# Rows of 1/rms through DRAM in place of TensorE's transposes, in a two-layer encoder

## The reference, cut to what matters

```
def rms_norm(x, g):
    y = x * rsqrt(mean(x * x, axis=-1) + EPS)
    return y * g
for l in range(2):
    x = x + hybrid_mixer(rms_norm(x, norm_mix_g[l]), ...)         # conv, attention, gMLP branches
    x = x + mem_cross_attention(rms_norm(x, norm_xattn_g[l]), mem, norm_mem_g[l], ...)
    x = x + conv_ffn(rms_norm(x, norm_ffn_g[l]), ...)             # up, depthwise conv, gate, down
return rms_norm(x, norm_final_g)
```

## Time and profile before

| | |
|---|---|
| median of 3 runs | 1756.15 us (1756.13 to 1756.55) |
| span of the profiled execution, first to last instruction | 1754.5 us |
| PE matmul busy | 1746.8 us, 8231 instructions |
| DVE busy | 1269.8 us |
| ACT busy | 744.8 us |
| POOL busy | 487.5 us |

### The profile page before, as it was taken

How to read it: one execution, slowest core, us unless ns; L and a number is a source line. 1 busy time by engine, 2 the same in 40 slices (tenths; PEclk the granted TensorE clock), 3 DMA queues, 4 the chain that set the end, 5 groups by cost and what they waited for, 6 DMA issues and landing times.

```text
span 1754.5 us, 21902 instructions
## 1 busy us (share of the span) xinstructions
PE 1746.8 (100%) x8231; PEld 1454.1 (83%) x8231; DVE 1269.8 (72%) x1688; ACT 744.8 (42%) x967; POOL 487.5 (28%) x204
## 2 busy tenths in 40 slices
PE   9999999999999999999999999999999999999998
PEld 7888888888888888888888888888888888888888
DVE  7998767573678777577779787665746797585585
ACT  4234654343564443343432345543445544343343
POOL 4453000103034244444133620010030333444440
PEclk9999999999999999999999999999999999999999
DMA  6532222322322332232231312223222223322321
GB/s 216 192 120 73 103 103 96 127 90 97 119 82 87 122 116 79 98 115 85 107 144 72 145 69 106 103 97 120 97 97 96 97 99 118 121 72 97 120 75 70
DMA packets 30698, 185.97 MB, mean 106 GB/s; under 512 B 3709, under 2 KB 6013, under 8 KB 10241
## 3 DMA queue, kind: packets, MB, share of 16 engines
q1 hardware_dynamic: 28380, 172.71, 27.4%
q0 software_dynamic: 1648, 11.54, 1.7%
q10 hardware_dynamic: 564, 0.33, 0.1%
HBM read 179.25 MB, written 7.68 MB: 107 GB/s over the span
## 4 chain that ended last, share of the span: by engine, by line
PE 96%; DVE 2%; issue 1%; ACT 1%; POOL 0%; DVEq 0%; POOLq 0%; ACTq 0%
PE ps L1640 28%; PE ps L1656 28%; PE ps L1641 28%; PE ps L1582 2%; PE ps L1576 2%; PE ps L1575 2%; PE ps L1739 1%; PE ps L1759 1%; DVE merged L1202 1%; DVE x_tl L985 1%; PE ps L1751 0%; PE ps L1670 0%; PE ps L1891 0%; PE ps L1884 0%; PE ps L1885 0%
## 5 line engine op out<-in xcount | busy, mean ns | idle before, releaser
L1640 PE MATMUL ps<-x_hd,w_hd 128*128 128x512 f32 x1568 | 612.8, 391 | 0.2
L1641 PE MATMUL ps<-x_tl,w_hd 128*128 128x512 f32 x1568 | 610.4, 389 | 0.0
L566 POOL TENSOR_TENSOR w_tl<-raw,w_hd 128x2048 fp32r<-128x2048 f32 x79 | 366.1, 4634 | 534.4 <-ACT w_hd L684 400.7
L684 ACT ACTIVATE w_hd<-raw 128x2048 fp32r<-128x2048 f32 (+2 forms) x159 | 298.2, 1876 | 324.8 <-PE ps L1641 240.3
L1656 PE MATMUL ps<-x_hd,w_tl 128*128 128x512 f32 x1568 | 373.4, 389 | 0.0
L1640 PEld LDWEIGHTS ps<-x_hd,w_hd 128*128 128x128 f32 x1568 | 294.4, 188 | 62.5 <-issue 0.8
L1656 PEld LDWEIGHTS ps<-x_hd,w_tl 128*128 128x128 f32 x1568 | 294.1, 188 | 61.0
L1641 PEld LDWEIGHTS ps<-x_tl,w_hd 128*128 128x128 f32 x1568 | 294.4, 188 | 60.3
L1640 PE MATMUL ps<-ring_hd,w_hd 128*128 128x512 f32 (+1 forms) x640 | 241.1, 381 | 0.0
L1641 PE MATMUL ps<-ring_tl,w_hd 128*128 128x512 f32 (+1 forms) x640 | 239.8, 379 | 0.0
L1347 DVE SCALAR_TENSOR_TENSOR merged<-merged 128x512 f32<-128x512 f32 x44 | 183.3, 4166 | 20.7 <-ACT merged L684 20.3
(11 more groups left out here) (227 smaller groups left out, 1646.1 us busy)
## 6 DMA issues: line engine op xcount, KB each, us to landing
raw<-units SPq DMA_DIRECT2D x154, 1024.0 KB, 4.8
bias_t<-bias_tiles POOLq DMA_DIRECT2D x8, 256.0 KB, 5.5
cg<-mem_t POOLq DMA_DIRECT2D x2, 1024.0 KB, 6.8
resid<-x_t POOLq DMA_DIRECT2D x1, 2048.0 KB, 8.2
resid_dram<-resid POOLq DMA_DIRECT2D x1, 2048.0 KB, 9.1
resid<-resid_dram POOLq DMA_DIRECT2D x1, 2048.0 KB, 8.8
out<-resid SPq DMA_DIRECT2D x7, 256.0 KB, 2.7
resid<-x_t SPq DMA_DIRECT2D x3, 512.0 KB, 9.0
```

What stands on the lines that cost most here:

```text
L566: line.done(pool.tensor_tensor(w_tl[:, k % 2, :], raw[:, k % 2, :], w_hd[:, k % 2, :].bitcast(F32), ALU.subtract), of_unit("tail", g))
L684: line.done(act.activation(out, in_, func, **kw), *labels)
L1640: pe.matmul(dst, w_hd[:, slot, w], hd[:, src, :], start=kc == 0, stop=False)
L1641: i = pe.matmul(dst, w_hd[:, slot, w], tl[:, src, :], start=False, stop=False)
```

## The change

For seven of the eight such places (`n0` of layer 1, and `c`, `mem` and `r2` of both layers) PE's `spread` is left out. In its place SP writes the columns element by element to a row in DRAM (`row_dram`), waits until the write has landed, and reads the row back broadcast to all 128 partitions. DVE waits for the read's semaphore `row_in`. DVE's copies of `misc` at `n0` of layer 1 and at `r2` go, and `c_norm` and the memory's scaling read the row in SBUF (`tmp[:, 3, :]`). `ROW_AT` says ahead of which unit's load SP does it. Layer 0's `n0` and the final norm keep the transposes.

```
+ROW_AT = {(0, 19): "c", (0, 31): "mem", (0, 48): "r2", (1, 4): "n0", (1, 19): "c", (1, 31): "mem", (1, 48): "r2"}
+ROW_NUMBER = {(_l, _tag): _n + 1 for _n, ((_l, _), _tag) in enumerate(ROW_AT.items())}
...
+        row = tmp[:, 3, :]
+        ROW_TO = {"n0": (rs0, r0[:], TB), "c": (rs, row, TB), "mem": (rs, row, MB), "r2": (rs, r_all, TB)}
+        row_dram = nc.dram_tensor("row_dram", (2, S), F32).ap()
...
+            def spread_row(tag):
+                src, dst, n = ROW_TO[tag]
+                number = ROW_NUMBER[line.part, tag]
+                sp.wait_ge(gpsimd_done, line.at(f"{tag}_rs"))
+                sp.dma_start(row_dram[number % 2, 0:P * n].rearrange("(t p) -> p t", p=P), src[:, 0:n],
+                             allow_slow_non_contiguous=True).then_inc(row_out, 16)
+                sp.wait_ge(row_out, 16 * number)
+                sp.dma_start(dst[:, 0:P * n], row_dram[number % 2, 0:P * n].rearrange("(o s) -> o s", o=1)
+                             .to_broadcast([P, P * n])).then_inc(row_in, 16)
+
             for g in range(2, TOTAL):
+                line.begin(g // NU)
+                if divmod(g, NU) in ROW_AT:
+                    spread_row(ROW_AT[divmod(g, NU)])
                 sp.wait_ge(gpsimd_done if tail_by_pool(g - 2) else vector_done, line.at(of_unit("tail", g - 2)))
                 sp.dma_start(raw[:, g % 2, :], units[g]).then_inc(weights_in[g % 2], 16)
...
-                op(lambda: dve.tensor_copy(r0[:], misc), "n0_r", needs=("n0b",))
+                if l:
+                    dve.wait_ge(row_in, 16 * ROW_NUMBER[l, "n0"])
+                else:
+                    op(lambda: dve.tensor_copy(r0[:], misc), "n0_r", needs=("n0b",))
...
-                                op(lambda: dve.tensor_copy(r_all, misc), "n2_r", needs=("r2b",))
+                                dve.wait_ge(row_in, 16 * ROW_NUMBER[l, "r2"])
...
+                        dve.wait_ge(row_in, 16 * ROW_NUMBER[l, "c"])
...
-                            op(lambda: dve.tensor_tensor(view, view, misc, ALU.mult), f"c_norm{t}", needs=("cb",))
+                            op(lambda: dve.tensor_tensor(view, view, row, ALU.mult), f"c_norm{t}")
...
-                    if k == CLN + 2:
-                        spread("c", 4)
...
-                        spread("mem", MB)
...
-                    if k == 44:
-                        spread("r2", 4)
```

More of the change, by code:

```diff
@@ L170 @@
 SUMS_IN = (2, 0)
-SPREAD_AT = (None, 1)
 IN_UNIT_2 = (5, 7)
@@ L451, in build @@
         out_sent = sem("out_sent")
+        row_out, row_in = sem("row_out"), sem("row_in")
         vector_waited, gpsimd_waited = sem("vector_waited"), sem("gpsimd_waited")
@@ L1401, in _ @@
                            "mem_ms", needs=("mems",))
+                    if k in MEM_SPLIT:
+                        dve.wait_ge(row_in, 16 * ROW_NUMBER[l, "mem"])
                     for t0 in MEM_SPLIT.get(k, ()):
@@ L1404, in _ @@
                             op(lambda: dve.scalar_tensor_tensor(sq[:, t % 2, 0:MEM], memf[:, t, :], col(l, "g_mem", t),
-                                                                misc[:, 0:MEM], ALU.mult, ALU.mult), f"mem_src{t}",
-                               needs=("memb",))
+                                                                row[:, 0:MEM], ALU.mult, ALU.mult), f"mem_src{t}")
                         for t in (t0, t0 + 1):
@@ L1843, in _ @@
                                 conv_sums if k == CLN + 2 and e == FIRST_OF[k] else
-                                first_spread if k == SPREAD_AT[l] else None)
-                        sums_at = KD // 2 if k == 39 else 2 if sums is first_spread or g == 2 else None
+                                None)
+                        sums_at = KD // 2 if k == 39 else 2 if g == 2 else None
                         if (kind, arg) == ("sv", 0):
@@ L1860, in _ @@
                         column_sums("mem", (), mem_sums, MB)
-                    if k == 27:
-                        pe.wait_ge(vector_done, line.at("ot3"))
-                        spread("mem", MB)
                     if k == 36:
```

## The result

The changed kernel takes 1783.76 us (median of 4 runs, 1782.52 to 1785.12) against 1756.14 for the kernel before on the same chip: 1.0157 times as long, 95% interval 1.0144 to 1.0169. The forecast was 1755.9, with a range up to 1759.4. It is slower, in the direction of the rival "a slow scatter" and beyond that rival's own upper bound of 1768.

A forecast was written before the change was run, and what follows sets the result against it. PE, busy 96% of the span, was taken to bound the kernel. Removed transposes (−2.64 us) plus late rows at `r2` (+2.4) gave −0.2, a median of 1755.9 us, with a range of 1753.4 to 1759.4.

The forecast's parts named there:

- a slow scatter: Rival: 512 writes of 4 bytes cost more than the load in front hides; slower, 1759.7 to 1768 us; chance 0.13.
- landing of the element write: At `r2`, SP's write to DRAM lands at 529.2, 0.7 us behind the load; bounds 528.46 and 532.1.
- The queue in front: At `r2`, the write stands behind a load with 2.6 us still to run, so it lands no earlier than 528.46.
- The read: The 256 KB broadcast read of the row takes 2.9 us; bounds 2.7 and 3.7.
- R: Time from the end of POOL's power until DVE may use the row; 6.4 us at `r2`, bounds 5.4 and 10.1.
- the prediction's formula: Time is 1753.5 + 2 × (R − 5.2) + 1 to 2 × (R − 7.6), brackets below zero counted as zero.
- 5.2 at `r2`: R beyond which each us delays PE by one us per layer, at unit (0, 52); 2.4 us in all at R = 6.4.
- 7.6 at `c`: R beyond which PE stalls for the evacuation ahead of unit (0, 17), one us per us; cost 0 at R = 6.4.
- DVE's fixed cycle: Behind `r2`, DVE and ACT run 10.58 us a unit against PE's 10.9, so DVE regains only 0.3 us a unit.
- a stall in units 45 to 47: Sign of being wrong: PE already stalls there, behind `r2`, rather than near the start of unit 52.
- Off PE: Removed transposes take 2.64 us off PE: 0.44 at each `r2`, `c` and `n0`, 0.22 at each `mem`.
- the fourth rival: The 24 transposes cost PE their duration of 0.27 us each, 6.5 us off PE; 1752 us; chance 0.05.

The follow-up runs named there:

- early, read alone: Against early: SP also waits for the row's read to land before issuing the next load; 1754.83 us (ratio 0.999).
- after: The changed kernel itself, with seven rows written to DRAM element by element; 1783.76 us (ratio 1.0157).
- pieces of 16 bytes, other order: Against the changed kernel: each partition writes its four numbers as one 16-byte piece, so tokens stand in another order; 1757.75 us (ratio 1.0008).
- 512 apart: Against the changed kernel: the 4-byte writes go 512 bytes apart in DRAM, and the read takes a row of weights; 1756.64 us.
- 64 apart: As 512 apart, but the 4-byte writes go 64 bytes apart in DRAM; 1756.59 us.
- 16 apart: As 512 apart, but the 4-byte writes go 16 bytes apart in DRAM; 1758.87 us.
- all in pieces: Against the changed kernel: all seven rows written in 16-byte pieces (8 at `mem`) in right order, PE turning every fourth (second) token's sums; 1757.53 us (1.0007).
- early: Against all in pieces: SP makes each row one unit earlier in its order, with no load in front in the queue; 1757.92 us (ratio 1.0009).
- PE kept busy: Against the changed kernel: useless matmuls added where PE waits, 16 at `c` and 22 at `r2`; 1789.3 us (ratio 1.0195).
- nothing in front: Against the changed kernel: SP makes each row one unit earlier, so no load runs in the queue when the write is issued; 1793.54 us.
- row in SBUF: Against the changed kernel: columns go element by element to one SBUF partition, then a second DMA copies them to the other 127; 1802.85 us (1.0265).
- kernels that turn every fourth token: Against the changed kernel: PE turns every fourth token's sums (second at `mem`), so each partition writes neighbours as one piece; four kernels, 1757.53, 1755.13, 1757.92, 1754.83 us.

## Why the prediction was wrong, step by step

**The step that failed** is the landing of the element write: taken at 529.2, 3.4 us after its issue, with 532.1 as the upper bound from the load of 128 elements at 3.66 us. It is 8.6 (7.98 to 9.9), outside both bounds. That row was no neighbour in the sense that matters: it reads single elements from DRAM and writes to SBUF, while this one writes 16 numbers into each 64 bytes of DRAM, and there the runs with distances put 5.5 us. The queue in front, from which I drew the lower bound, is worth 1.4 us (2.8 against 1.4 with pieces). The read was mis-sized too: 4.2 to 6.1 at `r2` and `c` against 2.9, its bounds 2.7 and 3.7.

**The rest of the sum held.** With each execution's R (end of the power to DVE's first use, from the rows of POOL and DVE) the prediction's formula, one us per us beyond 5.2 at `r2` and beyond 7.6 at `c` in each layer, gives the column "sum", where its 1753.5 is replaced by 1754.5. That constant is fitted to the fastest kernel, so the first row below is no test of it; where the 1.0 lies is in the next paragraph.

| kernel | R at `c`, layers 0 and 1 | R at `r2` | sum | measured |
|---|---|---|---|---|
| early, read alone | 5.4, 6.8 | 5.3, 5.3 | 1754.7 | 1754.83 (profiled: 1755.68) |
| after | 14.7, 14.6 | 12.8, 12.4 | 1783.4 | 1783.76 |
| pieces of 16 bytes, other order | 6.4, 6.7 | 6.8, 7.0 | 1757.9 | 1757.75 |
| 512 apart | 6.5, 6.3 | 6.1, 6.3 | 1756.5 | 1756.64 |
| 64 apart | 6.5, 6.5 | 6.2, 6.5 | 1756.8 | 1756.59 |
| 16 apart | 6.9, 6.8 | 7.1, 7.1 | 1758.3 | 1758.87 |
| all in pieces | 6.9, 7.1 | 6.6, 6.3 | 1757.0 | 1757.53 |
| early | 7.1, 7.8 | 6.7, 6.8 | 1757.8 | 1757.92 |
| PE kept busy | 15.0, 14.9 | 13.5, 13.5 | 1785.8 | 1789.3 (profiled: 1787.21) |
| nothing in front | 14.9, 16.0 | 14.8, 14.9 | 1789.5 | 1793.54 |
| row in SBUF | 17.5, 17.7 | 17.1, 16.6 | 1797.8 | 1802.85 |

The sum comes within 0.6 us of the first eight. The last three are 3.5 to 5 us longer; of that 2.0 and 4.0 in the last two are a wait at `n0`, which their R of 18.6 and 21.6 there brings.

So one us per us, near the places 5.2 and 7.6, and DVE's fixed cycle (evacuations at 555.95 and 566.54 in the kernel after, 10.59 us) were right. With long rows the lateness shows first at unit 46 and at the attention product, which the prediction hadn't, and nothing is left for units 51 and 52; it named a stall in units 45 to 47 as a sign of being wrong. But these waits, and the slow clock behind them, use up the same delay: the kernel with PE kept busy showed the rest of it coming out at units 17, 51 and 52.

**Off PE, and the two bounds, place by place.** 2.64 us were predicted; the fastest kernel is 1.7 below the kernel before (0.2 to 3.3 by its interval). The start of each product, less the start of the same product in the trace of before, shows where PE gained and lost. In the kernels with the seven rows `n0` gains 0.46, `r2` (with short rows) 0.47, `mem` 0.23 and `c` of layer 1 0.41 to 0.45, as predicted. `c` of layer 0 gains 0.06 to 0.13 instead of 0.44, since without the transposes PE comes too early there for DVE's `s_sb`; in the kernel after:

```profile
191.26 1.31 PE L1776 MATMUL ps<-ident,s_sb 128*128 128x128 f32 x10 [0.15 <-DVE s_sb L1139]
```

So 2.4 us came off, and the size was right but for one place. The bounds were off by a little: with R from 5.3 to 7.1 PE loses R less 5.0 (4.96 to 5.01) at `r2` in both layers, so 5.2 was 0.2 too high; at `c`, with long rows, it loses R less 7.8 to 8.1 and not 7.6, but for the place where the clock fell again. With short rows 0.3 us from `c` of layer 0 and 0.4 from the bound at `r2` are most of the 1.0 in the formula's constant; in the kernels that turn every fourth token that turning, 0.25 in all, is the rest. At their duration, the fourth rival, the transposes would have given 6.5: that falls.

**`n0` and `mem`**: no wait in the kernel after, as predicted, `n0` with less to spare than thought. **The chance** of 0.13 for the slow scatter was too small for a DMA of which the trace of before had no row of its kind, and its bounds leaned on a row of another kind.

## What to carry to other kernels

A small DMA is priced by what its pieces do at the target: before moving a layout through DRAM element by element, let each partition hold neighbours and write them as one piece. A wait of an in-order engine should be followed to the later place where the delay comes out; several waits and a slow clock behind them can be one and the same delay. What stands behind a short transfer in its queue matters as much as what stands in front.

## What the runs showed of the hardware that was not expected

- 512 writes of 4 bytes from SBUF into 2 KB of DRAM land in 8 to 10 us though their packets run in 0.4 to 0.7 us (with nothing in front, and in the kernel after); at 64 bytes apart in 3.1 us, as pieces of 16 bytes in 2.8, into one partition of SBUF at `c` and `r2` in 2.5 to 3.3 for each 128. What in the memory makes them wait isn't shown.
- A copy of 254 KB from one partition of SBUF to 127, in this form, ran on what amounts to one of the 16 DMA engines (busy share 6.5%) and took 12.2 to 12.8 us; 256 KB broadcast from a row in DRAM to 128 partitions took 3.0 to 4.3 at `c` and `r2` in the kernels with short writes behind a load.
- A 1 MB load issued 0.37 us behind a 256 KB read in one queue made that read 5.3 us at `r2` instead of 3.9.
